# Modulation loads, filter inputs and norm steps of an encoder layer's opening, put in another order

## The reference

```
c_act = silu(c)
mod = c_act @ w_ada + b_ada            # sh1, sc1, g1, sh2, sc2, g2
h = modulate(rmsnorm(x, norm1_g), sh1, sc1)
proj = h @ w_in
...
# filters of the Hyena branch: no dependence on x
h = sin(f1 * (z @ w1 + b1))
h = sin(f2 * (h @ w2 + b2))
h = h @ w3 ...
```

## Time and profile before

| quantity | us |
|---|---|
| median of 3 runs | 1112.43 |
| lowest, highest | 1112.22, 1113.51 |
| profiled execution, device time | 1114.14 |
| profiled execution, span of its instructions | 1112.6 |
| PE busy | 1092.2 (98%) |
| DVE busy | 802.3 (72%) |
| ACT busy | 454.5 (41%) |
| POOL busy | 108.9 (10%) |

### The profile page before, as it was taken

The page is one execution under the profiler, slowest core; times in us unless marked ns, Lnnn a source line. Parts: engine busy times, 40 slices in busy tenths (PEclk is TensorE's granted clock), DMA queues, the critical chain, the costliest instruction groups (busy, mean ns, idle before and its releaser), DMA issues.

```text
span 1112.6 us, 16634 instructions
## 1 busy us (share of the span) xinstructions
PE 1092.2 (98%) x6304; PEld 1022.2 (92%) x6304; DVE 802.3 (72%) x1334; ACT 454.5 (41%) x792; POOL 108.9 (10%) x132
## 2 busy tenths in 40 slices
PE   6999999999999999999999999999999999999997
PEld 4787798888899999999899999999999999999886
DVE  5777699889388685556455777787978778788534
ACT  5631156665722322423246232253442526157414
POOL 2101200000334322000000000000000000000000
PEclk9999999999999999999999999999999999999998
DMA  9923454333332333753312331143333232222303
GB/s 345 394 86 117 154 189 143 129 127 114 119 123 105 119 104 124 282 153 108 110 57 95 125 121 57 57 152 99 111 103 106 95 109 91 87 76 76 95 19 115
DMA packets 45525, 138.85 MB, mean 125 GB/s; under 512 B 5051, under 2 KB 10635, under 8 KB 44556
## 3 DMA queue, kind: packets, MB, share of 16 engines
q1 hardware_dynamic: 29024, 80.21, 21.6%
q0 software_dynamic: 11376, 44.84, 11.3%
q10 hardware_dynamic: 5052, 12.81, 3.3%
HBM read 121.61 MB, written 15.74 MB: 123 GB/s over the span
## 4 chain that ended last, share of the span: by engine, by line
PE 93%; DVE 4%; DMA 1%; ACT 1%; issue 0%; ACTq 0%; DVEq 0%
PE acc_ps L750 39%; PE wk L1181 16%; PE acc_ps L1200 12%; PE acc_ps L832 12%; PE wk L1056 2%; PE acc_ps L839 1%; PE wk L991 1%; PE wk L980 1%; PE wk L970 1%; PE wk L1022 1%; PE wk L872 1%; PE wk L885 1%; DVE dot_out L1832 1%; DMA filt_zh<-in_t_z 1%; PE wk L803 1%; PE wk L890 1%
## 5 line engine op out<-in xcount | busy, mean ns | idle before, releaser
L750 PE MATMUL acc_ps<-act_hilo,w_hi 128*128 128x384 f32 x1504 | 332.5, 342 | 0.1
L750 PEld LDWEIGHTS acc_ps<-act_hilo,w_hi 128*128 128x128 f32 x1504 | 264.8, 189 | 18.8 <-issue 17.7
L750 PE MATMUL acc_ps<-act_hilo,w_lo 128*128 128x384 f32 x752 | 191.5, 335 | 0.0
L750 PEld LDWEIGHTS acc_ps<-act_hilo,w_lo 128*128 128x128 f32 x752 | 136.4, 188 | 0.0
L1200 PE MATMUL acc_ps<-hidden_hilo,act_hilo 128*128 128x384 f32 x768 | 134.6, 335 | 0.2
L1200 PEld LDWEIGHTS acc_ps<-hidden_hilo,act_hilo 128*128 128x128 f32 x768 | 133.2, 188 | 1.1 <-issue 1.1
L1741 DVE TENSOR_TENSOR w_lo<-w_raw,w_hi 128x1024 fp32r<-128x1024 f32 x61 | 76.3, 1252 | 55.1 <-ACT w_hi L1282 54.1
L1282 ACT ACTIVATE w_hi<-w_raw 128x1024 fp32r<-128x1024 f32 x61 | 64.2, 1053 | 44.3 <-PE acc_ps L750 40.9
L2198 DVE SCALAR_TENSOR_TENSOR xT<-acc_ps,modT,xT 128x512 f32<-128x512 f32 (+1 forms) x32 | 19.7, 617 | 59.7 <-PE acc_ps L832 59.5
L1832 DVE CUSTOM_DVE_ANT_0 dot_out<-dot_ring,c_rows,vecT 128x1024 f32<-128x1024 f32 x48 | 61.6, 1284 | 1.6 <-issue 0.6
L2323 DVE SCALAR_TENSOR_TENSOR xT<-acc_ps,modT,xT 128x384 f32<-128x384 f32 (+2 forms) x96 | 40.5, 478 | 28.8 <-PE acc_ps L1200 28.8
(11 more groups left out here) (301 smaller groups left out, 2026.4 us busy)
## 6 DMA issues: line engine op xcount, KB each, us to landing
w_raw<-in_w_pre SPq DMA_DIRECT2D x50, 512.0 KB, 3.5
dot_ring<-in_w_ada_cols POOLq DMA_DIRECT2D x48, 512.0 KB, 3.8
w_raw<-in_w_up SPq DMA_DIRECT2D x32, 512.0 KB, 3.7
w_raw<-in_w_down SPq DMA_DIRECT2D x16, 512.0 KB, 3.4
w_raw<-in_w_down_half SPq DMA_DIRECT2D x32, 256.0 KB, 2.7
spec<-filt_out POOLq DMA_DIRECT2D x12, 512.0 KB, 2.9
gate_spill<-gates_out ACTq DMA_DIRECT2D x16, 384.0 KB, 2.3
hy_spec<-spec SPq DMA_DIRECT2D x12, 512.0 KB, 5.6
```

Source lines behind the costliest of these rows:

```text
L750: mm = pe.matmul(acc_ps[:, slot, 512 * h:512 * h + HALF], w[:, k, :], src[:, x, k, HALF * h:HALF * h + HALF], start=(first and i == 0), st ...
```

## The change

It does five things. The loads of the four groups of modulation pieces are dealt to SP and POOL by odd and even number, and group 0 and group 1's pieces come ahead of weight tile 0 and 1 on SP. On ACT's queue z and fw12 are issued before the identity matrix. On PE filt_mlp(0) comes before turn_c, filt_mlp(1) takes the place of one pair of warm matmuls (and one further pair is dropped), mod_row(0, 0) and (0, 1) come ahead of norm_sum and the other six of group 0 behind it, and first(1, 0) moves ahead of mod_row(2), first(1, 1) ahead of mod_turn(2). On ACT the sine of layer 0 stands behind square(3), with the table set loaded ahead of it; the square root's set is loaded behind square(7) and the sine's again behind norm_hi(5); mod_rows(0) comes ahead of split_w(0), and split_w(1) behind mod_rows(1). On DVE the whole angle chain of layer 0 is woven into the first two norm_acc, and the first two steps of layer 1's angle stand around norm_rstd.

```
 SP
-            mod_load(sp, 1)
+            for p in (1, 3):
+                mod_load(sp, p)
             weights(0)
+            for p in (5, 7):
+                mod_load(sp, p)
             weights(1)
-            for p in range(5, 4 * MODS, 2):
+            for p in range(9, 4 * MODS, 2):
                 mod_load(sp, p)
 POOL
-            for p in (0, 2, 3, *range(4, 4 * MODS, 2)):
+            for p in range(0, 4 * MODS, 2):
                 mod_load(pool, p)
 PE
+            pe.wait_ge(ld_filt, 32)
+            filt_mlp(0)
             pe.wait_ge(ld_ident, 16)
             turn_c()
-            pe.wait_ge(ld_filt, 32)
-            filt_mlp(0)
             pe.wait_ge(ones_set, 2)
-            for k in range(2, KD - 1):
+            for k in range(2, 6):
                 pe.wait_ge(n_acc, k)
-                warm(2)
+                if k == 3:
+                    pe.wait_ge(f_sin, 1)
+                    filt_mlp(1)
+                else:
+                    warm(2)
+            for k in range(2):
+                mod_row(0, k)
             norm_sum(0)
-            for k in range(KD):
+            for k in range(2, KD):
                 mod_row(0, k)
             norm_spread(0)
             mod_turn(0)
-            for k in range(4):
-                mod_row(1, k)
-            pe.wait_ge(f_sin, 1)
-            filt_mlp(1)
-            for k in range(4, KD):
+            for k in range(KD):
                 mod_row(1, k)
             first(0, 0)
             mod_turn(1)
             first(0, 1)
+            first(1, 0)
             for k in range(KD):
                 mod_row(2, k)
-            first(1, 0)
+            first(1, 1)
             mod_turn(2)
             first(0, 2)
-            first(1, 1)
 ACT
+            act_e.dma_start(zh[0:33, :], a["t_z"]).then_inc(ld_filt, 16)
+            act_e.dma_start(fw12[:], a["filt_w12"]).then_inc(ld_filt, 16)
             act_e.dma_start(ident[:], a["t_ident"]).then_inc(ld_ident, 16)
-            act_e.dma_start(fw12[:], a["filt_w12"]).then_inc(ld_filt, 16)
-            act_e.dma_start(zh[0:33, :], a["t_z"]).then_inc(ld_filt, 16)
...
-            act_e.activation(rs[:, 0:1], epsc[:], ACT.Sqrt).then_inc(sqrt_set, 1)
+            act_e.activation(es[:, 0, 0:1], epsc[:], ACT.Sin)
...
-            for k in range(KD):
+            for k in range(4):
                 square(k)
+            act_e.wait_ge(f_arg, 1)
+            act_e.activation(h1[:], fb[0:64, :], ACT.Sin).then_inc(f_sin, 1)
+            for k in range(4, KD):
+                square(k)
+            act_e.activation(rs[:, 0:1], epsc[:], ACT.Sqrt).then_inc(sqrt_set, 1)
             act_e.wait_ge(sqrt_set, 1)
             norm_std(0)
-            act_e.activation(es[:, 0, 0:1], epsc[:], ACT.Sin)
+            mod_rows(0)
             split_w(0)
-            mod_rows(0)
-            split_w(1)
-            act_e.wait_ge(f_arg, 1)
-            act_e.activation(h1[:], fb[0:64, :], ACT.Sin).then_inc(f_sin, 1)
...
             mod_rows(1)
+            split_w(1)
...
             norm_hi(5)
+            act_e.activation(es[:, 0, 0:1], epsc[:], ACT.Sin)
 DVE
-            for k in range(KD):
-                norm_acc(k)
             arg_first(0)
             arg_turns(0)
+            norm_acc(0)
+            arg_rest(0)
+            norm_acc(1)
+            arg_clamp(0)
+            for k in range(2, KD):
+                norm_acc(k)
+            arg_first(1)
             norm_rstd(0)
-            arg_rest(0)
-            arg_clamp(0)
+            arg_turns(1)
...
             mod_out(1)
-            arg_first(1)
             split_w(1)
...
             norm_t(5)
-            arg_turns(1)
```

## The result

The changed kernel takes 1122.38 us (median of 6 runs, 1120.59 to 1124.27) against 1112.54 for the kernel before (6 runs): ratio 1.0089, 95% interval 1.0076 to 1.0103. It is slower by 9.8 us, where 2.9 were forecast. Its profiled execution has a span of 1121.9 us, 9.3 more than the profiled one before. Both profiled executions are among the longest of their kernels (1114.14 and 1124.27 us), so lengths read from the two traces lie at the upper end.

A forecast was written before the change was run, and what follows sets the result against it. PE, busy 98%, was taken to bound the kernel, so only the start of its unbroken block run counts: norm_h(0) 4.7 later, 2.4 won back, 0.6 for the clock, 2.9 us in all; 1115.3 us, range 1110.8 to 1118.2.

The forecast's parts named there:

- The three loads: ACT's queue: z by 3.5 us, fw12 at 5.5, identity at 9.5, putting square(0) at about 11.0 instead of 6.72.
- The woven chain: DVE: 5.7 us of angle work ahead of the third norm_acc completes the sum at 23.1, 4.4 us later.
- The clock until norm_sum: PE: half speed until 24.6, norm_sum ending at 26.3, norm_h(0) starting at 30.8, 4.7 us later.
- What is won back: norm_h(0) to the last turn: 17.6 us instead of 19.9, plus 0.6 for another clock fall; mod_turn(3) 2.9 later.
- PE's order: PE's middle: first(1, 0) at 38.0 to 39.1, then mod_row(2) to 40.9, chained at full clock.
- The loads, the sine's table: SP, POOL and ACT: later pieces cost nothing; the sine's table reload costs nothing, up to 1.5 us if uncovered.
- slow to the end: Rival, chance 0.12: PE stays at 1.2 GHz through norm_sum, rows, spread and turn, some 3 us more, 1118.
- the half-speed filt_mlp(1): Clock sign on PE: passes of 512 columns at L848 lie 0.85 us apart.
- a later stretch at half clock: Clock sign on PE: a stretch at 0.5 granted clock between 34 and 42 us.
- c_turned: Sign on ACT: the copy of the turned c at L1353 comes near 10 us.
- the run: Sign on PE: the unbroken run of blocks starts at 48 to 49 us.

The follow-up runs named there:

- queue_only: Kernel before with z and fw12 ahead of the identity on ACT's queue and filt_mlp(0) ahead of turn_c: 1115.69 us, ratio 1.0029.
- filter_back: Changed kernel with the filter's chain unwoven again, DVE doing all eight norm_acc before the angle: 1118.49 us, ratio 1.0055.
- fq_back: filter_back with the identity first on ACT's queue again and turn_c ahead of filt_mlp(0): 1115.04 us, ratio 1.0018.
- c_later: Changed kernel with ACT's copy of the turned c behind square(2): 1123.27 us, ratio 1.0088.
- weave_queue: Kernel before with the new ACT queue order and the whole woven filter chain, without the other parts: 1121.32 us, ratio 1.0080.
- kept_warm: Changed kernel with six more warm matmuls on PE behind turn_c: 1120.75 us, ratio 1.0080.
- fewer_warm: Changed kernel without the two warm pairs behind filt_mlp(1): 1124.96 us, ratio 1.0116.
- mid_warm: kept_warm with five more warm matmuls between mod_row(1) and first(0, 0): 1119.47 us, ratio 1.0072.
- peord_only: Kernel before with only PE's middle order changed, first(1, 0) ahead of mod_row(2) and first(1, 1) ahead of mod_turn(2): 1115.24 us, ratio 1.0016.
- peord_back: Changed kernel with PE's order in the middle as before: 1122.51 us, ratio 1.0077.
- fqp_back: fq_back with PE's order of blocks in the middle also as before: 1113.30 us, ratio 1.0008.
- best: t3_first with one warm pair less, the changed loads, and ACT's mod_rows(0), split_w(1) and mod_rows(1) reordered: 1112.37 us, ratio 0.9997.
- t3_first: Kernel before with norm_t(3) ahead of arg_first(1) and split_w(1) on DVE: 1111.16 us, ratio 0.9983.
- loads_only: Kernel before with only SP's and POOL's order of modulation pieces and weight tiles changed: 1121.64 us, ratio 1.0086.

## Why the prediction was wrong

The direction, and where to look, held: the end moved with the beginning of the run of blocks, 7.9 of 9.3 us. The size did not, nor the range.

1. *The three loads.* fw12 was taken at 5.5 and came at 8.1, the identity at 9.5 and came at 11.07. Both lie in their bounds. Together they put the last norm_acc at 24.42 instead of 23.1: a mis-sized term, 1.3 us. Of their price alone, queue_only says 3 us, and so does the step from filter_back to fq_back (5.9 over the kernel before against 2.9); with the weave in place c_later finds only 0.3 us of it in the sum.
2. *The woven chain.* Right in mechanism: the sum is 5.7 us late, 4.4 forecast. Without the weave it is 2.7 us late (filter_back, 21.45), so the weave itself adds 3.0 to it. On the time, undoing it gives back about 4 us (filter_back), adding it costs about 6 over queue_only (weave_queue).
3. *The clock until norm_sum.* "I take it as slow until 24.6": it was slow until 26.9. norm_sum started at 27.28 instead of 25.0. Of these 2.3 us, 1.3 are the later sine (filt_mlp(1) at 19.26, forecast 18.0) and 1.0 is the half speed; kept_warm, with PE busy, starts norm_sum at 24.36. From there to norm_h(0) another 0.5 us is missing in the forecast, so norm_h(0) is 7.4 us late and not 4.7. The high end given, slow throughout, is what fewer_warm shows.
4. *What is won back.* This is the step that failed; items 1 and 3 are terms mis-sized on the way to norm_h(0). I wrote 17.6 us "worked out at full clock" and put 0.6 us on another fall. Measured are 20.4 us, none of the 2.4 won back. The fall lasted 6.8 us instead of 3.4 and lay over the turn and three blocks in a row on the path to mod_rows(2). mid_warm, which fills the 2.1 us pause, has the clock up there and 18.4 us. So the fall costs 2.0 to 2.4 us (20.4 and kept_warm's 20.8 against 18.4) where 0.6 was put, and the chain at full clock was 0.8 too short. The pause I had seen; its price I took as a fraction of the fall before, when PE now stood in front of a longer one with more behind it.
5. *PE's order.* I chained first(1, 0) ahead of mod_row(2) at full clock and gave the step no price of its own. peord_only says 2 us on the kernel before, most of it from a fall twice as long; in the changed kernel, where the fall is there anyhow, peord_back finds 0.7 us, inside the 20.4.
6. *The loads, the sine's table.* The loads were free in the changed kernel, as said: its mod_row(2) starts at 44.25 and waits for no piece. The prediction added that 35 would be the next wait if the norm were not late, and that came true in fqp_back and best. The second load of the sine's set ends at 54.91 while norm_h(6) starts at 55.02, just behind mod_out(3). So the load fitted into the idle time, as the rows had it. The drain that the Trainium skill adds to it (ScalarE: Activation LUTs, What ACT_TABLE_LOAD costs) does not show here either. The overrun that the prediction estimates at 1.1 us by the Trainium skill's figure is 1.2 by its own terms (1.28 + 0.20 + 1.4 - 1.68).

Of the rivals, "slow to the end" came nearest in number (1118), but its mechanism did not come: norm_sum, rows, spread and turn took 1.50, 1.91, 1.60 and 0.95 us, as at full speed. The half speed lay ahead of them and behind them. Of the 5 us missed at the last turn, 2.8 arose up to norm_h(0) and 2.2 from there on. Of the signs named ahead, the half-speed filt_mlp(1) and a later stretch at half clock came; c_turned (11.76), the last norm_acc (24.42), norm_h(0) (33.58) and the run (54.0) all lay beyond the places given.

The sum of parts: undone one after the other, each kernel's median against that of the kernel before beside it, the excess goes from 9.8 us to 5.9 without the weave, to 2.9 without the queue's order too, and to 1.2 without PE's order. That makes about 4 for the weave, 3 for the queue, 2 for PE's order and 1 for the rest, which the ratio of fqp_back can't tell from nothing. Added to the kernel before, queue and PE's order come out alike (3 and 2), the weave at 6: its price differs by what it stands beside.

## What to carry to other kernels

Where PE idles a microsecond or two among small matmuls in a latency-bound opening, price the fall of its clock over everything that follows on the path, not as a share of the fall seen before; moving one line so that the pause goes (t3_first) made the kernel faster, which none of the change's own edits did. One profiled execution does not say how often such a fall comes: the kernel before seems to have it in fewer than half of its executions. Work moved into an engine's idle time must fit behind what that time is waiting for: DVE's 5.7 us cost nothing behind the last norm_acc; ahead of it they made the sum 3.0 us later and the whole 4 to 6. And an order of loads is only as good as the order in which the consuming engine asks for them: the same edit cost about 1 us with ACT's order moved (fqp_back) and 9.6 without (loads_only).

## What the runs showed that I had not expected

Some 4.6 to 7 more microseconds of idle filler work on PE made the opening shorter: kept_warm's run begins 2.5 us earlier than the changed kernel's, mid_warm's 3.6; in the traces only, since on the whole time neither gain is clear of the spread. In the middle of the opening the granted clock fell to half (0.51, the 1.2 GHz level) at pauses of 1.12 to 2.11 us: for 3.4 us in the kernel before and queue_only, for 6.8 in the changed one, peord_only, fq_back and others. With pauses of at most 0.61 us it did not fall (t3_first, fqp_back). But the pause alone does not decide it. mid_warm's fall at 26.7 came 2.7 us behind a pause of 0.78 us that kept_warm had too, without a fall there, and of the kernel before's 71 executions 40 have a higher mean clock and less time, as if it had not fallen. At the start of a program the granted clock column reads 1.00 while passes of 256 columns lie 0.4 us apart, against 0.23 later: there it has to be read from the passes. And a transfer of 64 KB on ACT's queue lands at 3.3 us if issued at 0.9, at 11.1 if issued at 2.2.
